# Attention steps taken from two heads in turn and weighed as a pair, and a VectorE update placed ahead of the next head's preparation

## The chip, the cores and the metric

The kernel runs on one core of one Trainium2 chip. It is one program for a whole model: a first block of two layers and a second block of two layers, 512 tokens wide 1024. The metric is the device time of one execution in microseconds (us), the median of several runs. The engines are TensorE (PE in the profile; its weight loads are PEld), VectorE (DVE), ScalarE (ACT), GpSimd (POOL) and SyncE (SP), which here only issues DMAs.

## The reference, cut to what matters

The change lies in the mixer of the second block, which runs once in each of its two layers. The mixer has a convolution (done elsewhere), a differential attention of 6 heads and a gated delta rule of 6 heads. What is computed for them:

```python
def diff_attention(q, k, v, lam_q1, ..., subln_w, layer_idx):   # 6 heads, 2 maps per head, 4 blocks of 128 rows
    ...
    def block(args):
        q_blk, blk = args
        s = jnp.einsum("bqmd,bkmd->bmqk", q_blk, kf)
        ...
        p = jax.nn.softmax(s - slopes[:, None, None] * dist, axis=-1)
        p = p.reshape(B, H, 2, Q_BLOCK, S)
        a = p[:, :, 0] - lam * p[:, :, 1]
        return jnp.einsum("bhqk,bkhe->bqhe", a, vf)

def chunk_gated_delta(q, k, v, g, beta):                        # 6 heads, two directions, chunks of 64
    ...
    decay = jnp.exp(jnp.where(lower, gc[..., :, None] - gc[..., None, :], -jnp.inf))
    A = jnp.where(strict, jnp.einsum("bhncd,bhnsd->bhncs", kb, kc) * decay, 0.0)
    sol = lax.linalg.triangular_solve(A, rhs, left_side=True, lower=True, unit_diagonal=True)
    ...
    def step(state, inp):
        v_new = u_i - jnp.einsum("bhcd,bhde->bhce", w_i, state)
        o = jnp.einsum("bhcd,bhde->bhce", qg_i, state) + jnp.einsum("bhcs,bhse->bhce", aqk_i, v_new)
        state = state * gl_i[..., None, None] + jnp.einsum("bhcd,bhce->bhde", kdec_i, v_new)
```

## The kernel before

`mixer_stage` writes the order of each engine out by hand. Engines run in program order, and semaphores tie them together. The loop goes over 49 slots, t = 7h + lv: for each of the 6 delta heads h it has 7 levels lv, in which the inverse of the triangular matrix is built up by doubling, and a last row of 7 slots (h = 6) that only finishes what is behind. The loop of a slot has, on each engine, pieces of three pipelines:

- **The levels.** TensorE turns the present inverse (`turn`, L3283) and multiplies it with a masked block (`pairs`, L3267). ScalarE copies both results out of PSUM (`turned_copy` L3491, `pairs_copy` L3495). TensorE multiplies the copies (`products`, L3292). VectorE subtracts the product (`update`, L3808 and L3809; L3801 at level 6), and the next slot's `turn` waits for that. GpSimd makes the masked blocks (`masked_level`, L3656).
- **The next head's preparation and the last head's recurrence.** VectorE takes `low` (L3763), `exponents` (L3769 for the first direction, L3772 for the second) and `queries` (L3777) for head h + 1 at levels 2 to 5; ScalarE follows with `decay_exp` (L3478) and `low_exp` (L3472), which stand in its order ahead of the next slot's copies. For head h - 1, TensorE runs `values` (L3318), `results` (L3332, L3337) and `states_seen` (L3303); VectorE `values` (the copy L3823), `states` and `corrected`. `results` of level 4 waits for the copy that VectorE makes at the end of level 3. TensorE runs `before(h, lv)` ahead of `products` and `behind(h, lv)` behind it.
- **The attention steps.** There are 24 steps, one for a head and a block of 128 rows, numbered head by head. Step s begins in slot begins[s] = 7h + 2i + 2. Then, by lag: lag 0 `scores` (L3383, two matmuls from the stacked queries and keys of its head); lag 1 `top` on VectorE and `exps` on ScalarE (L3543); lag 2 `invert`, `rescale` (L3549), `subtract` (L3751); lag 3 `turn_step` (L3393), four transposes in two parts with ScalarE's `copy` between them (L3555); lag 4 `weigh` (L3400), four matmuls of 128x64 weights with 128 columns, and `out` on ScalarE (L3560). `weigh` and the first part of `turn_step` stand between `pairs` and `products`; `scores` and the second part stand behind `products`. Weights of 64 columns fill one half of TensorE's columns: even heads the lower, odd heads the upper, by `half(h)`. fp32 matmuls show as two records each.

The stacked operands lie in two buffers, by h % 2. SyncE fills one with 12 DMAs of 64 KB (L3226), when the scores that read its last content are done: for h >= 2, `sp.wait_ge(scored, 8 * (h - 1))`.

`core.hold` (L242) adds matmuls whose results nobody reads; it stands in slots 1 to 4 and in the last 7.

In the slots of level 5 from head 1 on (t = 12, 19, ...) the weighing of one step and the first transposes of another meet, and the transposes wait for `out`, since both share bank 7.

Of the kernel before, what the change touches and what calls it, by code (L numbers as in the profile page):

```python
# [1066 lines left out]
class Modulation:  # L1067
# [19 lines left out]
    def sum(self, q, n):  # L1087
        return self.core.sb(self.sums[q % len(self.sums)] + n * MOD_W, MOD_W)
# [1688 lines left out]
def u2(core, t):  # L2777
    return core.sb(U0 + t * SEQ, SEQ)
# [330 lines left out]
def mixer_stage(core, nc, a, l, pl):  # L3109
# [22 lines left out]
    ds_bank = lambda d, hh: core.ps[hh, 4, 2 * P + d * HD:2 * P + (d + 1) * HD]  # L3132
    score_bank = lambda m: core.ps[:, 5 + m, :]
    turn_bank = core.ps[:, 7, 0:2 * P]
    weigh_bank = lambda hh: core.ps[hh, 7, 2 * P:3 * P]
    level_of = lambda h, lv: h * LV + lv
    masked_of = lambda h, lv: h * (LV - 1) + lv
    moved_at = lambda h, lv: h * (2 * LV - 1) + 2 * lv + 1
# [47 lines left out]
    def half(h):  # L3186
        return slice((h % 2) * HD, (h % 2 + 1) * HD)
# [1 line left out]
    def order(d):  # L3189
        return range(4) if d == 0 else range(3, -1, -1)  # L3190

    steps = [(h, i) for h in range(6) for i in range(4)]
    N = len(steps)
    slots = LV * (H + 1)
    split_at = {LV - 1: 1, 3 * LV - 1: 2}
# [1 line left out]
    sc = lambda s, c, w=2: core.sb(GX0 + (s % 2) * 8 + c, w)  # L3197
    tiles_of = lambda n, t: u2(core, 4 + 3 * n + t)

    begins = [LV * h + 2 * i + 2 for h, i in steps]  # L3200

    def step_at(t, lag):

        return begins.index(t - lag) if t - lag in begins else None

    kv_bank = lambda b: core.ps[:, (4, 3, 1)[b % 3], :]
    kv_at = lambda b: c4(pl.kt if b < 3 else pl.vt)[:, :, (b % 3) * P:(b % 3 + 1) * P]

    with nc.Block() as block:
        @block.sync  # L3210
        def _(sp):
            sp.dma_start(pl.pairs, core.const("pairs")).then_inc(loads_in, 16)
            sp.dma_start(pl.dist, core.const("dist")).then_inc(loads_in, 16)
            for n, name in enumerate(("diff_lambda_q1_2", "diff_lambda_k1_2", "diff_lambda_q2_2", "diff_lambda_k2_2")):
                sp.dma_start(pl.lamv[:, n * 32:(n + 1) * 32], a[name][l].partition_broadcast(P)).then_inc(loads_in, 16)
            for h in range(H):
                t = h // 2
                sp.wait_ge(pair_low, 2 * t + 2)
                if h >= 2:
                    sp.wait_ge(scored, 8 * (h - 1))  # L3220
                parts = [(pl.high[n].bitcast(F32), tiles_of(n, t)) for n in range(2)]
                for m in range(2):
                    mp = (2 * h + m) % 4
                    for n, (high, low) in enumerate(parts):
                        for place, src in enumerate(((low, high, high), (high, low, high))[n]):
                            sp.dma_start(pl.stack[h % 2][m][n][place * DD:(place + 1) * DD].bitcast(F32),  # L3226
                                         src[mp * DD:(mp + 1) * DD]).then_inc(stack_in[h % 2], 16)

        @block.tensor
        def _(pe):  # L3230
# [154 lines left out]
            def turn_step(s, part):  # L3385
                if part == 0:
                    pe.wait_ge(subtracted, s + 1)
                    if s:
                        pe.wait_ge(out_done, s)
                else:  # L3390
                    pe.wait_ge(turned_copied, 2 * s + 1)
                for j in range(2):
                    mm = nc.tensor.transpose(turn_bank[:, cc(j)], pl.both[s % 2][:, cc(2 * part + j)], core.ident())  # L3393
                mm.then_inc(turned, 1)

            def weigh(s):
                h, i = steps[s]
                pe.wait_ge(turned_copied, 2 * s + 2)
                for j in range(4):
                    mm = nc.tensor.matmul(weigh_bank(half(h)), pl.vt_diff[:, j * DIFF_W + h * HD:j * DIFF_W + (h + 1) * HD],  # L3400
                                          pl.at[s % 2][:, cc(j)], start=(j == 0), stop=(j == 3))
                mm.then_inc(weighted, 1)

            def attend(t, place):

                if place == 0:
                    for s, work in ((step_at(t, 4), weigh), (step_at(t, 3), lambda s: turn_step(s, 0))):
                        if s is not None:
                            work(s)
                else:  # L3410
                    for s, work in ((step_at(t, 0), scores), (step_at(t, 3), lambda s: turn_step(s, 1))):
                        if s is not None:
                            work(s)
# [48 lines left out]
        def _(act):  # L3462
# [88 lines left out]
            def copy(s, part):  # L3551
                act.wait_ge(turned, 2 * s + part + 1)
                if part == 0 and s >= 2:
                    act.wait_ge(weighted, s - 1)
                nc.scalar.activation(pl.at[s % 2][:, two(part)], turn_bank, ACT.Copy).then_inc(turned_copied, 1)  # L3555

            def out(s):
                h, i = steps[s]
                act.wait_ge(weighted, s + 1)
                nc.scalar.activation(u2(core, 4 + h // 2)[half(h), cc(i)], weigh_bank(half(h)), ACT.Copy).then_inc(out_done, 1)  # L3560

            row_exp(0, 0)
            split(0)
# [13 lines left out]
            for t in range(slots):  # L3577
                h, lv = divmod(t, LV)
                if step_at(t, 4) is not None:
                    copy(step_at(t, 4), 1)  # L3580
                if h < H and lv:
                    turned_copy(h, lv)
                    pairs_copy(h, lv)
                    if lv < LV - 1:
                        save(h, lv)
                    else:
                        full(h)
                    if lv == 5 and h < H - 1:
                        near(h + 1)
                if step_at(t, 2) is not None:  # L3590
                    rescale(step_at(t, 2))
                if step_at(t, 4) is not None:
                    out(step_at(t, 4))
                if step_at(t, 3) is not None:
                    copy(step_at(t, 3), 0)
                if step_at(t, 1) is not None:
                    exps(step_at(t, 1))
                if t in split_at:
                    split(split_at[t])
                if lv == 0 and h > 1:  # L3600
                    outputs(h - 2)
                if h < H - 1 and lv in (1, 2, 3):
                    prepare(h + 1, lv - 1)
# [100 lines left out]
        def _(dve):  # L3704
# [106 lines left out]
            def corrected(h, n):  # L3811
                dve.wait_ge(seen, 3 * h + n)
                for d in range(2):
                    R, c = pl.run[d], order(d)[n]
                    rv = R["rv"][h % 2][:, ch(c)]
                    dve.wait_ge(ops_done, 2 * h + d + 1)
                    nc.vector.scalar_tensor_tensor(out=rv, in0=seen_bank(d), scalar=cols(pl.nbge, h, d)[:, c:c + 1], in1=rv,
                                                   op0=ALU.mult, op1=ALU.add).then_inc(rv_done, 1)
# [43 lines left out]
            for t in range(slots):  # L3862
                h, lv = divmod(t, LV)
                ahead = h < H - 1
                if step_at(t, 1) is not None:
                    top(step_at(t, 1))
                if step_at(t, 2) is not None:
                    invert(step_at(t, 2))
                if h:
                    if lv in (0, 2, 5):  # L3870
                        values(h - 1, (0, 2, 5).index(lv) if lv < 5 else 3)
                    if lv in (1, 4):
                        states(h - 1, (0, 2)[lv // 4])
                    if lv == 3:
                        corrected(h - 1, 2)
                if ahead and lv == 2:
                    low(h + 1, 0)
                    exponents(h + 1, 0)
                if ahead and lv == 3:
                    low(h + 1, 1)  # L3880
                    exponents(h + 1, 1)
                if ahead and lv in (4, 5):
                    queries(h + 1, lv - 4)
                if h < H and t:
                    update(h, lv)
                if t == 1:
                    query_gram(0)
                    lambdas_difference()
                if t in (2, 3):
                    queries(0, t - 2)  # L3890
                if step_at(t, 2) is not None:
                    subtract(step_at(t, 2))
                if ahead and lv in (1, 2):
                    differences(h + 1, lv - 1)
                if h:
                    if lv in (1, 4):
                        corrected(h - 1, (1, 3)[lv // 4])
                    if lv == 2:
                        states(h - 1, 1)
                    if lv == 3:  # L3900
                        values(h - 1, 2)
                if ahead and lv == 4:
                    key_gram(h + 1)
                if ahead and lv == 5:
                    query_gram(h + 1)
                if t in split_at:
                    split(split_at[t])
# [129 lines left out]
```

## Time and profile before

| what | value |
|---|---|
| median of 3 runs | 3773.4 us (3767.73 to 3790.59) |
| the profiled execution's own time | 3768.21 us |
| its span | 3766.4 us, 58660 instructions |
| mean granted TensorE clock | 0.989 |
| PE / DVE / ACT / POOL busy | 97% / 57% / 41% / 9% |

The span is the time from the first to the last instruction. The profiled execution lies near the fastest of the runs, 5 us below their median. Clock 1.00 is 2.4 GHz, 0.50 is 1.2 GHz. A matmul's time in the profile goes from its start to its modelled end; consecutive ones overlap, so the distance between starts is what they cost.

### The profile page before, as it was taken

What the parts mean: (1) busy time and instruction counts of PE and PEld (TensorE: products, weight loads), DVE (VectorE), ACT (ScalarE), POOL (GpSimd) and SP (SyncE); (2) the same over time, 40 slices, a digit from 0 to 9 for tenths busy, and PEclk for the clock granted to TensorE, in tenths of its full rate; (3) what the DMA queues carried; (4) which work ended last, traced back from release to release, by engine and by line L of the source; (5) the groups of instructions that cost most, each with busy time, mean ns of one, the idle gap of its engine ahead of it and who ended that gap; (6) DMA issues with size and microseconds to landing.
All of it is one profiled execution on the core that took longest, in us unless ns stands there. A gap on an engine that the chain in (4) does not pass through costs nothing. (4 is left out here: it accounts for less than half of the span.)

```text
span 3766.4 us, 58660 instructions
## 1 busy us (share of the span) xinstructions
PE 3642.5 (97%) x24921; PEld 3014.7 (80%) x24921; DVE 2162.8 (57%) x3353; ACT 1537.2 (41%) x2423; POOL 335.0 (9%) x325
## 2 busy tenths in 40 slices
PE   7999899999999999999999998999999998999998
PEld 4887688888888888878888777777888777778887
DVE  4734766455466444465227776755367867644375
ACT  3224633111354322354226435643266436633364
POOL 0030220000000000000000005410000015310000
PEclk9999999999999999999999999999999999999999
DMA  5530013333212111122323311113232311022231
GB/s 194 176 109 5 7 46 112 124 123 123 87 62 69 62 57 65 65 79 90 100 89 101 91 56 35 28 46 101 79 111 90 91 47 31 20 90 79 90 101 67
DMA packets 262767, 301.24 MB, mean 80 GB/s; under 512 B 9371, under 2 KB 229426, under 8 KB 262514
## 3 DMA queue, kind: packets, MB, share of 16 engines
q1 hardware_dynamic: 260433, 293.41, 24.3%
q8 instruction: 190, 3.11, 0.3%
q10 hardware_dynamic: 2080, 4.19, 0.3%
q14 instruction: 64, 0.52, 0.0%
HBM read 284.14 MB, written 2.10 MB: 76 GB/s over the span
## 5 line engine op out<-in xcount | busy, mean ns | idle before, releaser
L536 PE MATMUL banks<-h_halves,w_halves 128*128 128x512 f32 x3708 | 1370.8, 370 | 14.1 <-DVEq L428 10.6
L538 PE MATMUL banks<-h_halves,w_halves 128*128 128x512 f32 x3708 | 1365.0, 368 | 0.0
L540 PE MATMUL banks<-h_halves,w_halves 128*128 128x512 f32 x3708 | 1359.6, 367 | 0.0
L536 PEld LDWEIGHTS banks<-h_halves,w_halves 128*128 128x128 f32 x3708 | 699.0, 189 | 146.8 <-issue 13.8
L540 PEld LDWEIGHTS banks<-h_halves,w_halves 128*128 128x128 f32 x3708 | 697.5, 188 | 118.5
L538 PEld LDWEIGHTS banks<-h_halves,w_halves 128*128 128x128 f32 x3708 | 698.7, 188 | 115.6 <-issue 1.4
L263 DVE TENSOR_TENSOR w_halves<-work,w_halves 128x2048 fp32r<-128x2048 f32 (+1 forms) x212 | 482.5, 2276 | 486.0 <-ACT w_halves L258 485.9
L258 ACT ACTIVATE w_halves<-work 128x2048 fp32r<-128x2048 f32 (+1 forms) x212 | 401.8, 1895 | 387.4 <-PE banks L540 363.6
L258 ACT ACTIVATE h_halves<-kept 128x512 fp32r<-128x512 f32 (+1 forms) x520 | 332.8, 666 | 282.3 <-PE banks L540 235.6
L263 DVE TENSOR_TENSOR h_halves<-kept,h_halves 128x512 fp32r<-128x512 f32 (+1 forms) x514 | 356.8, 735 | 137.4 <-ACT h_halves L258 136.3
L1130 DVE SCALAR_TENSOR_TENSOR kept<-kept 128x512 f32<-128x512 f32 x280 | 189.8, 749 | 9.9 <-DMA kept<-in_mod_w 9.9
L884 ACT ACTIVATE kept<-banks 128x512 f32<-128x512 f32 x66 | 30.0, 530 | 242.0 <-PE banks L540 242.0
L1510 POOL TENSOR_TENSOR h_halves<-kept,h_halves 128x768 fp32r<-128x768 f32 (+1 forms) x8 | 13.7, 1712 | 1282.3 <-ACT kept L1477 1282.3
L869 ACT ACTIVATE kept<-kept 128x512 f32<-128x512 f32 x64 | 37.6, 632 | 213.9 <-DVE kept L863 213.9
L2480 PE MATMUL banks<-h_halves,w_halves 128*128 128x512 f32 x320 | 119.8, 374 | 1.2 <-DVE h_halves L1484 0.8
L2481 PE MATMUL banks<-h_halves,w_halves 128*128 128x512 f32 x320 | 118.2, 369 | 0.0
L242 PE MATMUL banks<-kept 128*1 128x128 f32 x914 | 113.3, 276 | 4.9 <-DVE work L2294 4.9
L2482 PE MATMUL banks<-h_halves,w_halves 128*128 128x512 f32 x320 | 117.8, 368 | 0.0
L863 DVE SCALAR_TENSOR_TENSOR kept<-banks,kept 128x512 f32<-128x512 f32 x64 | 41.4, 685 | 122.4 <-PE banks L540 122.3
L2498 PE MATMUL banks<-w_halves,h_halves 128*128 128x256 f32 x384 | 108.7, 283 | 0.0
L2497 PE MATMUL banks<-w_halves,h_halves 128*128 128x256 f32 x384 | 108.7, 283 | 0.0
L2496 PE MATMUL banks<-w_halves,h_halves 128*128 128x256 f32 x384 | 108.7, 283 | 0.0
(415 smaller groups left out, 4685.3 us busy)
## 6 DMA issues: line engine op xcount, KB each, us to landing
work<-in_w_ff SPq DMA_DIRECT2D x64, 1024.0 KB, 5.3
work<-in_ffn_w_in SPq DMA_DIRECT2D x44, 1024.0 KB, 5.1
kept<-in_mod_w SPq DMA_DIRECT2D x40, 1024.0 KB, 5.1
work<-in_odd_w_in SPq DMA_DIRECT2D x24, 1024.0 KB, 5.2
work<-in_w_in SPq DMA_DIRECT2D x24, 1024.0 KB, 5.2
work<-in_ffn_w_out SPq DMA_DIRECT2D x16, 1024.0 KB, 5.3
work<-in_even_w_in SPq DMA_DIRECT2D x13, 1024.0 KB, 5.3
work<-in_odd_w_out SPq DMA_DIRECT2D x8, 1024.0 KB, 5.3
```

Source lines behind the costliest of these rows:

```text
L242: self.nc.tensor.matmul(self.ps[0:1, bank, 0:P], self.sb(ONES0, 1), self.ident(), start=True, stop=True)
L258: return core.nc.scalar.activation(dst, src, ACT.Copy)
L263: return core.nc.vector.tensor_tensor(dst, src, high.bitcast(F32), ALU.subtract)
L536: nc.tensor.matmul(o, low[:, k - a, fc], rh[:, tc], start=opens, stop=False, skip_group_check=shared)
L538: nc.tensor.matmul(o, high[:, k - a, fc], rl[:, tc], start=False, stop=False, skip_group_check=shared)
L540: mm = nc.tensor.matmul(o, high[:, k - a, fc], rh[:, tc], start=False, stop=(k == K - 1), skip_group_check=shared)
L1130: ins = nc.vector.scalar_tensor_tensor(out=self.sum(q, n), in0=self.slot(m)[:, k], scalar=c, in1=self.sum(q, n), op0=ALU.mult, op1=ALU.add)
L2480: nc.tensor.matmul(o, low[:, c, fc], rh, start=(c == 0), stop=False)
L2481: nc.tensor.matmul(o, high[:, c, fc], rl, start=False, stop=False)
L2482: mm = nc.tensor.matmul(o, high[:, c, fc], rh, start=False, stop=(c == KD - 1))
L2496: nc.tensor.matmul(o, core.h(c, 1)[:, tc], high[:, c, :], start=(c == 0), stop=False)
L2497: nc.tensor.matmul(o, core.h(c)[:, tc], low[:, c, :], start=False, stop=False)
```

## The change

The 24 steps are numbered so that the two heads of a pair take turns: step s is block i of head 2b + e, in the order b, i, e. The slots in which steps begin are the same numbers as before. An odd step's slot of lag 4 weighs its own and the preceding step: eight matmuls, alternating between the two column halves, and one `out` of 128 partitions in place of two of 64. The slots of lag 4 of even steps (7q + 6, level 6, and 7q + 10, level 3, for q = 0 to 5) have no `weigh` and no `out` any more. Both heads of a pair must be stacked before the second step, and SyncE's wait for a free buffer becomes step (h - 2, 3)'s scores in the new order. On VectorE, `update` moves ahead of `low`, `exponents` and `queries` of the next head, in levels 2 to 5.

```diff
-    weigh_bank = lambda hh: core.ps[hh, 7, 2 * P:3 * P]
+    weigh_bank = core.ps[:, 7, 2 * P:3 * P]
...
-    steps = [(h, i) for h in range(6) for i in range(4)]
+    steps = [(2 * b + e, i) for b in range(3) for i in range(4) for e in range(2)]
...
-    begins = [LV * h + 2 * i + 2 for h, i in steps]
+    begins = [LV * (s // 4) + 2 * (s % 4) + 2 for s in range(N)]
+    weighed_before = lambda s: sum(1 for n in range(1, N, 2) if begins[n] + 4 <= begins[s] + 3)
...
+    def odd_step(t, lag):
+
+        s = step_at(t, lag)
+        return s if s is not None and s % 2 else None
...
-                    sp.wait_ge(scored, 8 * (h - 1))
+                    sp.wait_ge(scored, 2 * steps.index((h - 2, 3)) + 2)
...
             def turn_step(s, part):
                 if part == 0:
                     pe.wait_ge(subtracted, s + 1)
-                    if s:
-                        pe.wait_ge(out_done, s)
+                    if weighed_before(s):
+                        pe.wait_ge(out_done, weighed_before(s))
...
             def weigh(s):
-                h, i = steps[s]
                 pe.wait_ge(turned_copied, 2 * s + 2)
                 for j in range(4):
-                    mm = nc.tensor.matmul(weigh_bank(half(h)), pl.vt_diff[:, j * DIFF_W + h * HD:j * DIFF_W + (h + 1) * HD],
-                                          pl.at[s % 2][:, cc(j)], start=(j == 0), stop=(j == 3))
+                    for n in (s - 1, s):
+                        h, i = steps[n]
+                        mm = nc.tensor.matmul(weigh_bank[half(h)], pl.vt_diff[:, j * DIFF_W + h * HD:j * DIFF_W + (h + 1) * HD],
+                                              pl.at[n % 2][:, cc(j)], start=(j == 0), stop=(j == 3))
                 mm.then_inc(weighted, 1)
...
-                act.wait_ge(weighted, s + 1)
-                nc.scalar.activation(u2(core, 4 + h // 2)[half(h), cc(i)], weigh_bank(half(h)), ACT.Copy).then_inc(out_done, 1)
+                act.wait_ge(weighted, s // 2 + 1)
+                nc.scalar.activation(u2(core, 4 + h // 2)[:, cc(i)], weigh_bank, ACT.Copy).then_inc(out_done, 1)
...
-                if step_at(t, 4) is not None:
-                    out(step_at(t, 4))
+                if odd_step(t, 4) is not None:
+                    out(odd_step(t, 4))
...
+                if h < H and t:
+                    update(h, lv)
                 if ahead and lv == 2:
                     low(h + 1, 0)
                     exponents(h + 1, 0)
...
                 if ahead and lv in (4, 5):
                     queries(h + 1, lv - 4)
-                if h < H and t:
-                    update(h, lv)
```

## Rows read from the trace of the kernel before

**Rows 1.** The page: busy time, share of the span, instructions, by engine.

```profile
PE 3642.5 (97%) x24921; PEld 3014.7 (80%) x24921; DVE 2162.8 (57%) x3353; ACT 1537.2 (41%) x2423; POOL 335.0 (9%) x325
```

**Rows 2.** Windows: length, busy PE, PEld, DVE, ACT, POOL; clock; DMA; the first mixer.

```profile
2268.00:2496.00 228.00, 209.45 (x3781) 166.58 (x3782) 151.31 (x458) 140.01 (x368) 98.52 (x121) 0.97 0.11 26
```

**Rows 3.** Timeline of PE, mixer of the first block: start, duration, line, tile, records.

```profile
349.20 1.09 PE L2013 MATMUL banks<-work,kept 128*64 128x128 f32 x16
```

**Rows 4.** Timeline of PE, head 2, levels 5 and 6; idle time and releaser in brackets.

```profile
2372.05 0.41 PE L3393 MATMUL banks<-kept 128*128 128x128 f32 x2 [0.45 <-ACT kept L3560]
...
2375.95 1.09 PE L3400 MATMUL banks<-work,kept 128*64 128x128 f32 x8
2376.96 0.68 PE L3292 MATMUL banks<-work 64*64 64x64 f32 x16
```

**Rows 5.** Timeline of ACT, head 2, level 6.

```profile
2376.06 0.38 ACT L3495 ACTIVATE work<-banks 128x256 f32<-128x256 f32 x1
```

**Rows 6.** Timeline of PE, head 2, levels 3 and 4.

```profile
2361.71 0.45 PE L3292 MATMUL banks<-work 32*32 32x32 f32 x32
2362.16 0.66 PE L3318 MATMUL banks<-work 128*128 128x64 f32 x4
2363.79 0.45 PE L3283 MATMUL banks<-kept,work 32*32 32x32 f32 x32 [0.97 <-DVE work L3808]
...
2364.92 0.45 PE L3332 MATMUL banks<-work 128*64 128x64 f32 x4 [0.37 <-DVE work L3823]
```

**Rows 7.** Timeline of DVE, head 2, level 3.

```profile
2362.02 0.92 DVE L3763 TENSOR_SCALAR work<-work 128x512 f32<-128x512 f32 x1
2362.86 0.68 DVE L3772 SCALAR_TENSOR_TENSOR work<-work 128x512 f32<-128x512 f32 x1
2363.46 0.27 DVE L3808 TENSOR_TENSOR work<-work,banks 128x128 f32<-128x128 f32 x1
...
2363.86 0.74 DVE L3751 SCALAR_TENSOR_TENSOR kept<-kept 128x512 f32<-128x512 f32 x1
2364.52 0.34 DVE L3823 COPY work<-banks 128x64 f32<-128x64 f32 x2
```

**Rows 8.** Timeline of POOL, head 2, level 3.

```profile
2361.93 0.73 POOL L3656 TENSOR_TENSOR work<-work 128x256 f32<-128x256 f32 x1
```

**Rows 9.** Timeline of DVE, head 5, level 3.

```profile
2458.09 0.29 DVE L3808 TENSOR_TENSOR work<-work,banks 128x128 f32<-128x128 f32 x1 [0.96 <-PE banks L3292]
```

**Rows 10.** Timeline of ACT, head 0, level 3.

```profile
2295.45 0.63 ACT L3478 ACTIVATE work<-work 128x512 f32<-128x512 f32 x1 [0.25 <-DVE work L3772]
```

**Rows 11.** Timeline of PE, the last seven slots, slot 45.

```profile
2483.34 1.09 PE L3400 MATMUL banks<-work,kept 128*64 128x128 f32 x8
2484.36 0.82 PE L242 MATMUL banks<-kept 128*1 128x128 f32 x6
```

**Rows 12.** Windows: head 1 (levels 3 to 4, then 4 to 5), head 2 (3 to 4).

```profile
2323.30:2328.60 5.30, 3.91 (x119) 3.39 (x120) 5.01 (x19) 4.37 (x13) 3.61 (x5) 1.00 0.42 102
2328.60:2338.90 10.30, 10.30 (x97) 8.60 (x96) 5.78 (x16) 3.42 (x10) 5.34 (x7) 0.50 0.01 2
2360.10:2365.40 5.30, 3.95 (x118) 3.35 (x119) 5.01 (x18) 4.08 (x12) 2.97 (x5) 1.00 0.38 91
```

**Rows 13.** Timeline of PE, head 1, levels 4 and 5.

```profile
2328.08 0.45 PE L3332 MATMUL banks<-work 128*64 128x64 f32 x4 [0.37 <-DVE work L3823]
...
2339.73 0.41 PE L3393 MATMUL banks<-kept 128*128 128x128 f32 x2 [0.45 <-ACT kept L3560]
```

**Rows 14.** Timeline of SP's queue: first and last issues of one head's stack.

```profile
2354.95 1.82 SPq L3226 DMA_DIRECT2D p_halves<-kept  x3
...
2363.09 0.58 SPq L3226 DMA_DIRECT2D p_halves<-work  x1
```

**Rows 15.** DMA issues by line: count, KB each, median us from issue to landing.

```profile
p_halves<-kept SPq DMA_DIRECT2D x48, 64.0 KB, 2.0
```

**Rows 16.** Timeline of PE: the scores of slots 13 and 16.

```profile
2346.56 0.73 PE L3383 MATMUL banks<-p_halves 96*128 96x512 f32 x2
...
2358.07 0.73 PE L3383 MATMUL banks<-p_halves 96*128 96x512 f32 x2
```

More of the change, by code:

```diff
@@ L3406, in attend @@
                 if place == 0:
-                    for s, work in ((step_at(t, 4), weigh), (step_at(t, 3), lambda s: turn_step(s, 0))):
-                        if s is not None:
-                            work(s)
+                    if odd_step(t, 4) is not None:
+                        weigh(odd_step(t, 4))
+                    if step_at(t, 3) is not None:
+                        turn_step(step_at(t, 3), 0)
                 else:
@@ L3553, in copy @@
                 if part == 0 and s >= 2:
-                    act.wait_ge(weighted, s - 1)
+                    act.wait_ge(weighted, s // 2)
                 nc.scalar.activation(pl.at[s % 2][:, two(part)], turn_bank, ACT.Copy).then_inc(turned_copied, 1)
@@ L3591, in _ @@
                     rescale(step_at(t, 2))
-                if step_at(t, 4) is not None:
-                    out(step_at(t, 4))
+                if odd_step(t, 4) is not None:
+                    out(odd_step(t, 4))
                 if step_at(t, 3) is not None:
```

## The prediction, made before the result was known

> **What bounds the kernel now.** I read the page first: TensorE is busy for 97% of the span [rows 1]. The windows of the first mixer say how much of that the change can reach: a stage of 228 us, with TensorE busy 209 of them, at a mean clock of 0.97 [rows 2]; the second mixer is a like stage. 1% of the kernel is 37.7 us, so an eighth of one mixer. About 1% is also what a measurement of this kernel can tell from no change. Then I read the timeline slot by slot, on all engines, for one head, and asked at each `products` and each `turn` what it had waited for.
>
> Levels 4, 5, 6, 0, 1 and the start of 2 go mostly at TensorE's own pace: its instructions follow each other, and what is taken out there shortens the slot, until ScalarE's copies come last. Level 3 and the start of level 4 do not. There TensorE stands for 0.97 us until `update` is done, and 0.37 us more until VectorE has made the copy L3823 [rows 6]. VectorE has no gap in that stretch: L3763, L3772, `update`, `subtract` and the copy follow end to end [rows 7]. So in level 3 of heads 1 to 4, which all have this form, VectorE sets the pace.
>
> **The weighing itself.** A pair takes eight matmuls in place of twice four. The first block's mixer already weighs two heads in alternating column halves: 16 records in 1.09 us [rows 3]. One head here takes 8 records in the same 1.09 us [rows 4]. I take the pair at 1.09 us: the weighings that stay (levels 1 and 5) cost what they did, and 12 weighings in each mixer are gone. The other bound is that nothing overlaps, 1.0 us more at each of 24 pairs. The Trainium skill, "TensorEngine Tiling (Array Packing)", section "Key Properties", says that changing the tiling mode drains the engine. Modes alternate between neighbours in both kernels, and by that rule a removed weighing would give back a drain too; no row here separates one, and the sum leaves it out.
>
> **Level 6, six in each mixer.** `products` started at 2376.96, behind the weighing that began at 2375.95 [rows 4]. Without it the next thing to wait for is ScalarE's copy of the pairs, which ended at 2376.44 [rows 5]. So 0.5 us of the 1.0 come out, 12 x 0.5 = 6.0 us. Bounds 0.4 and 1.0 each.
>
> **Level 3, heads 1 to 4, eight in all.** `products` would start 1.0 us earlier than 2361.71 [rows 6], but VectorE is still at work until 2362.02 [rows 7]. `update` now comes first there and is done at 2362.4, so TensorE turns and pairs at once. Then it meets `results`, which waits for the copy L3823. Its place in VectorE's order is unchanged, behind `low`, `exponents`, `update` and `subtract` in whichever order, and these add up to the same 2.5 us. So the wait for `update` becomes a wait for the copy, and the gain of both halves of the change is nothing here. One small term is left: L3763 ran beside GpSimd's L3656 from 2362.02 to 2362.66 and took 0.92 us [rows 7, 8]; 0.4 us later it meets it for 0.24 us only. I take 0.3 us each (0 to 0.4): 2.4 us.
>
> **Level 3, head 5, two in all.** No next head is prepared; VectorE waited 0.96 us for `products` [rows 9], and gets them a weighing earlier: 2 x 0.95 = 1.9 us.
>
> **The last seven slots.** TensorE runs from the weighing into fillers without a gap [rows 11]: 2 x 1.0 = 2.0 us.
>
> **Head 0.** ScalarE's `decay_exp` already waited 0.25 us for `exponents` [rows 10], and the next slot's two copies stand behind it. `exponents` now stands behind `update`, which waits for `products`: 0.4 us of `update` and 0.1 to 0.4 us of waiting. I charge 0.5 us in each mixer, 1.0 us (0 to 2).
>
> **The rest of the moved order, at nothing.** In levels 2, 4 and 5, `update` comes up to 0.6 us sooner, but TensorE did not wait for it; `queries` comes later, and its readers are a slot away. ScalarE loses twelve `out` of 0.27 us in each mixer; nothing waits for them but the transposes of level 5 [rows 4], and that one stays.
>
> **SyncE's loads.** Heads 0 and 1 are stacked back to back before slot 4, as the 24 issues already stand. For heads 2 and 4 the release moves from slot 8 (22) to slot 13 (27), while the first use stays at slot 16 (30). From the end of the scores of slot 13 to those of slot 16 there were 10.8 us [rows 16]. The load takes 8.1 us from first to last issue and 2.0 us to land [rows 14, 15], 10.1 us. That fits by 0.6 us, where it had several slots to spare before, and the odd head's load queues behind it with about the same margin. TensorE would stand with everything behind `scores`. For heads 2 to 5 of both mixers I charge 1 us in sum (0 to 5).
>
> Together: -6.0 - 2.4 - 1.9 - 2.0 + 1.0 + 1.0 = -10.3 us, if the clock does what it did.
>
> **The clock.** I don't think it will. In head 1 the granted clock fell to 0.50 (1.2 GHz) at 2328.6 and stayed there for 10.3 us [rows 12]; what TensorE had done before was the level 3 pattern, 3.91 us busy of 5.3. In head 2 the same stretch with 3.95 us of 5.3 passed at 1.00. The second mixer shows the same: a fall behind level 3 of head 1, none in heads 2 to 4. So two of eight such stretches fall, and the others stand close to it. The change takes the 1.0 us of the weighing out of just this stretch while its length, VectorE's, stays: idle time rises from 1.35 to about 2.4 us, and what is left is mostly 32x32 tiles. The price is in the rows: from `results` of level 4 to the first transposes of level 5, head 1 took 11.65 us [rows 13] and head 2 took 7.13 us [rows 4, 6], so 4.5 us. I expect five of the other six stretches to fall: +22.5 us. The Trainium skill, "TensorE: Matmul & The Clock Gate", section "HAM oscillation — how this bites in real kernels", tells of kernels whose engine drops to the lower clock again and again through idle gaps between bursts; this speaks against taking work out of a stretch that another engine sets, and by it the further falls come. In rows 12 one stretch agrees and one does not.
>
> **The sum.** The profiled execution took 3768.2 us. 3768.2 - 10.3 + 22.5 = 3780.4 us. The median of the runs lies 5.2 us above the profiled time; I add half of that and forecast 3783 us.
>
> **Rivals.**
> - The clock holds: TensorE's idle time in level 3 rises, but the clock falls only where it did. For it: three of four heads passed at 1.00 with a quarter of the stretch idle, and head 0 has longer gaps. Against it: the near equality of two stretches of which one fell [rows 12]. It gives 3768 - 10 = 3758 to 3763 us. Chance 0.32.
> - The stacks come late: from a load time of 10.8 us on, every further us is paid at heads 2 and 4, and again for heads 3 and 5, at the worst 1.2 us at eight places, about 8 us above the rest: 3768 to 3772 us with the clock as before. Chance 0.08.
> - The eight matmuls do not overlap: +1.0 us at the 24 pairs against the sum of -10.3 us, and fuller stretches for the clock: about 3782 us. Rows 3 speak against it. Chance 0.04.
> - Slower by over 1%: the clock falls in all eight stretches and, head 0 being slower too, in both of its, and once more in each head, since a stretch at 1.2 GHz moves what comes after it: 14 further falls x 4.5 = 63 us, minus 10. It decides from some ten further falls on. 3811 us and above. Chance 0.04.
> - Faster by over 1% would need four times the sum: 0.01.
> - My forecast, 3 to 7 further falls, 3771 to 3790 us: 0.51.
>
> The likeliest case gives the time. Its own range is 3771 to 3792 us. The range for 8 in 10 has to take in the case in which the clock holds, and on the other side eight falls with late stacks: 3756 to 3797 us. In chances: slower by over 1% 0.05, faster by over 1% 0.01, within 1% 0.94.
>
> **What would show it.** In the timeline of the changed kernel: L3400 with x16 in 1.09 us at levels 1 and 5 only; L3292 of level 6 starting right at the end of L3495; in level 4 of heads 1 to 4 no wait of L3283 for L3808, but some 1.5 us of L3332 for L3823; L3383 of slots 16 and 30 waiting for the queue if the stacks are late. In the windows: clock 0.50 behind level 3 of heads 2 to 4. I am wrong if VectorE's stretch in level 3 gets shorter by more than 0.5 us, or if the mixers' mean clock stays at 0.97.

## The result, and the profile after

The changed kernel is slower: 3792.3 us median (3787.4 to 3810.76, 20 runs) against 3773.2 us (3767.5 to 3790.6, 20 runs), ratio 1.0043, 95% interval 1.0031 to 1.0054. The forecast was 3783 us, range 3756 to 3797. Its profiled execution has a span of 3791.1 us against 3766.4.

The page's line of busy times answers to [rows 1], the windows of both mixers to [rows 2].

```profile
PE 3654.7 (96%) x24921; PEld 3022.2 (80%) x24921; DVE 2158.8 (57%) x3353; ACT 1531.9 (40%) x2399; POOL 336.5 (9%) x325
```

```profile
2271.00:2509.00 238.00, 212.08 (x3788) 168.17 (x3789) 151.36 (x463) 138.18 (x359) 99.48 (x121) 0.90 0.10 25
3108.00:3344.00 236.00, 213.99 (x3737) 168.95 (x3734) 145.09 (x453) 132.67 (x349) 93.83 (x115) 0.86 0.09 22
```

ScalarE has 24 instructions fewer, TensorE the same number. The mixers' mean clock went from 0.97 to 0.90 and 0.86. From the scores of slot 2 to the first matmul of the next stage the first mixer took 206.4 us before and 213.8 after, the second 205.9 and 219.8. So 21.3 of the 24.7 us are there. The other 3.4 us lie ahead of the first mixer, in code that did not change. They look like a difference between executions: the scores of slot 2 of the first mixer start at 2291.2 us in the profiled execution of the kernel before, and at 2292.2 to 2298.4 us in those of all other kernels here.

TensorE's timeline for levels 3 to 6 of head 2 answers to [rows 4, 6]. `products` is now L3298, `values` L3324, `turn` L3289, `results` L3338, `weigh` L3407, `scores` L3389.

```profile
2361.52 0.73 PE L3389 MATMUL banks<-p_halves 96*128 96x512 f32 x2
...
2365.61 0.66 PE L3324 MATMUL banks<-work 128*128 128x64 f32 x4 [1.01 <-DVE work L3825]
2366.20 0.45 PE L3289 MATMUL banks<-kept,work 32*32 32x32 f32 x32
...
2367.97 0.69 PE L3338 MATMUL banks<-work 128*64 128x64 f32 x4 [0.91 <-DVE work L3831]
...
2377.46 1.09 PE L3407 MATMUL banks<-work,kept 128*64 128x128 f32 x16
2379.02 0.41 PE L3399 MATMUL banks<-kept 128*128 128x128 f32 x2 [0.47 <-ACT kept L3568]
...
2383.47 0.68 PE L3298 MATMUL banks<-work 64*64 64x64 f32 x16 [0.48 <-ACT work L3503]
```

`turn` no longer waits for `update`; `results` waits 0.91 us for VectorE's copy, and `values`, which stands ahead of `turn`, waits 1.01 us for `corrected` (L3825): 1.9 us idle where 1.34 were. The pair takes 16 records in 1.09 us. In level 6, `products` waits for ScalarE's copy. VectorE's timeline of level 3 answers to [rows 7]: the same instructions end to end, `update` (L3816) first, the copy (L3831) last.

```profile
2365.09 0.47 DVE L3825 SCALAR_TENSOR_TENSOR work<-banks,kept,work 128x64 f32<-128x64 f32 x2
2365.47 0.28 DVE L3816 TENSOR_TENSOR work<-work,banks 128x128 f32<-128x128 f32 x1
...
2365.86 0.52 DVE L3771 TENSOR_SCALAR work<-work 128x512 f32<-128x512 f32 x1
2366.31 0.68 DVE L3780 SCALAR_TENSOR_TENSOR work<-work 128x512 f32<-128x512 f32 x1
2366.91 0.74 DVE L3759 SCALAR_TENSOR_TENSOR kept<-kept 128x512 f32<-128x512 f32 x1
2367.57 0.34 DVE L3831 COPY work<-banks 128x64 f32<-128x64 f32 x2
```

The windows up to the fall of the clock and behind it, head 2 and head 3, answer to [rows 12] (the clock is the third number from the end).

```profile
2361.50:2366.70 5.20, 3.79 (x165) 3.11 (x168) 4.32 (x15) 3.99 (x12) 3.12 (x4) 1.00 0.34 80
2366.70:2376.90 10.20, 9.29 (x119) 7.56 (x107) 6.44 (x19) 4.18 (x11) 5.26 (x6) 0.50 0.12 29
2398.90:2404.20 5.30, 3.18 (x131) 2.71 (x120) 5.01 (x20) 4.31 (x12) 3.55 (x5) 1.00 0.01 3
2404.20:2414.40 10.20, 10.20 (x101) 8.49 (x101) 5.23 (x15) 3.49 (x10) 5.28 (x7) 0.50 0.01 2
```

The clock fell behind level 3 of heads 1, 2, 3 and 4, in both mixers: eight falls, two before. In the second mixer it was low once more in head 0, for 23.9 us from 3131.2 on.

In heads 1, 2 and 4 of both mixers, six of the eight, the clock was low before the wait of `results` began: in head 2 from 2366.7 on, while that wait runs from 2367.1 to 2367.97. By then TensorE had missed the weighing and stood for 1.4 us of 5.2 us, most of it in front of `values`; in head 2 of the kernel before it stood for 1.35 us of 5.3 us, and the clock stayed at 1.00 [rows 12]. So the 1.9 us of both waits are not what brought the clock down, and the idle time alone does not tell the stretches that fell from those that passed.

### The profile page after: what moved, and what is told of

Read it like the earlier page. It is cut to its first block and busy times, and to the rows that moved or that the text cites. A ratio compares the mean times of both kernels' runs of the same rounds, so it can differ in the third digit from the quotient of the medians.

```text
span 3791.1 us, 58634 instructions
## 1 busy us (share of the span) xinstructions
PE 3654.7 (96%) x24921; PEld 3022.2 (80%) x24921; DVE 2158.8 (57%) x3353; ACT 1531.9 (40%) x2399; POOL 336.5 (9%) x325
## 5 line engine op out<-in xcount | busy, mean ns | idle before, releaser
L536 PE MATMUL banks<-h_halves,w_halves 128*128 128x512 f32 x3708 | 1370.5, 370 | 14.0 <-DVEq L428 10.6
L536 PEld LDWEIGHTS banks<-h_halves,w_halves 128*128 128x128 f32 x3708 | 699.0, 189 | 145.9 <-issue 13.7
L1510 POOL TENSOR_TENSOR h_halves<-kept,h_halves 128x768 fp32r<-128x768 f32 (+1 forms) x8 | 13.7, 1713 | 1282.6 <-ACT kept L1477 1282.6
```

What stands on the lines that cost most here:

```text
L536: nc.tensor.matmul(o, low[:, k - a, fc], rh[:, tc], start=opens, stop=False, skip_group_check=shared)
```

## The experiments

Two theories. **Clock:** TensorE's missing microsecond in level 3 makes the granted clock fall there, and the falls are the whole loss. **Order:** the new waits (for VectorE's copy, for `exponents`, for the stacks) are the loss, and the clock goes along. The table has every run; "falls" are stretches at 0.50 that begin behind level 3 of heads 1 to 4, of eight in a profiled execution.

The falls are counted in one execution of each kernel, and executions differ. The mean granted clock of every execution bears the counts out: 0.971 to 0.980 in the changed kernel and 0.969 to 0.977 in e2; 0.988 to 0.991 in e1, 0.987 to 0.991 in e8 and 0.986 to 0.991 in e4; 0.978 to 0.991 in 85 executions of the kernel before, whose profiled execution, at 0.989, lies above its median of 0.987. It thus shows less low clock than most executions of that kernel have.

| kernel | weighing in level 3 | fillers | falls | median us | ratio to before, interval |
|---|---|---|---|---|---|
| before | yes | no | 2 | 3773 to 3776 | |
| changed | no | no | 8 | 3792.3 | 1.0043 (1.0031 to 1.0054) |
| e1 changed | no | 4 and 3 | 0 | 3760.4 | 0.9952 (0.9934 to 0.997) |
| e2 pairs only | no | no | 8 | 3808.2 | 1.0076 (1.005 to 1.0102) |
| e3 `update` only | yes | no | 1 | 3777.5 | 1.0002 (0.9984 to 1.002) |
| e4 before | yes | 3 and 1 | 0 | 3763.7 | 0.9973 (0.9956 to 0.999) |
| e5 changed | no | 4 and 3, more | 0 | 3751.1 | 0.994 (0.9917 to 0.9962) |
| e6 as e1, one head after the other | no | 4 and 3 | 0 | 3767.1 | 0.9976 (0.9956 to 0.9995) |
| e7 order only | yes | no | 3 | 3790.0 | 1.0043 (1.0016 to 1.0069) |
| e8 changed | no | 4 | 0 | 3756.5 | 0.995 (0.9929 to 0.997) |
| e9 as e7 | yes | 3 and 1 | 0 | 3762.7 | 0.9969 (0.9957 to 0.9981) |
| e10 as e2 | no | 4 and 3, more | 0 | 3753.0 | 0.9945 (0.9929 to 0.9961) |
| e11 changed | no | 2 | 3 | 3785.3 | 1.0032 (1.0011 to 1.0053) |
| e12 changed | no | 4, more | 0 | 3754.8 | 0.9953 (0.9934 to 0.9973) |

**e1, the changed kernel with fillers.** A filler is a matmul of one weight column whose result nobody reads, as `core.hold` has them, in a free part of bank 7.

```diff
+            def fill(n):
+                for _ in range(n):
+                    nc.tensor.matmul(core.ps[0:1, 7, 3 * P:4 * P], core.sb(ONES0, 1), core.ident(), start=True, stop=True)
...
                         pairs(h, lv)
+                    if 1 <= h <= 4 and lv == 4:
+                        fill(3)
                     before(h, lv)
...
                         products(h, lv)
+                    if 1 <= h <= 4 and lv == 3:
+                        fill(4)
                     behind(h, lv)
```

> The changed kernel with fillers on TensorE where it now stands idle: four filler matmuls behind `products` of level 3 and three ahead of `results` of level 4, for heads 1 to 4 (about 1.0 and 0.8 us, in gaps of 1.0 and 0.9 us). Clock theory: the granted clock stays at 1.00 behind level 3 of heads 1 to 4; the seven or eight falls there are gone, at 3.5 to 4.5 us each, so 3792 - 30 = 3758 to 3768 us, below the kernel before (ratio 0.996 to 0.999). Rival, in which the new waits in the order (for VectorE's copy, for `exponents`, for the stacks) carry the loss and the clock only goes along: the fillers fill idle time and nothing else moves, 3790 to 3795 us.

Measured 3760.4 us: 32 us off the changed kernel and 0.5% under the one before, by adding work. TensorE's timeline in head 2, fillers at L3433:

```profile
2363.13 1.03 PE L3433 MATMUL banks<-kept 128*1 128x128 f32 x8
2364.21 0.66 PE L3324 MATMUL banks<-work 128*128 128x64 f32 x4
...
2365.49 0.81 PE L3433 MATMUL banks<-kept 128*1 128x128 f32 x6
2366.58 0.45 PE L3338 MATMUL banks<-work 128*64 128x64 f32 x4 [0.28 <-DVE work L3839]
```

and the same windows as above:

```profile
2360.10:2365.40 5.30, 4.85 (x181) 3.79 (x180) 4.41 (x15) 4.09 (x12) 3.13 (x4) 1.00 0.34 80
2365.40:2375.60 10.20, 9.45 (x160) 7.68 (x146) 7.46 (x24) 6.93 (x20) 6.21 (x8) 1.00 0.12 29
```

From the scores of slot 16 to `results` of level 4 it is 6.46 us, as in the changed kernel (2361.52 to 2367.97): the fillers bought no time there. They kept the clock behind it. The order theory gave 3790 to 3795 us and is refuted as the cause of the loss. Elsewhere the clock was not quite held: in e1 it fell once in head 5, for 10.2 us, and in head 0 of both mixers.

**e2, pairs only:** `update` back behind `low`, `exponents` and `queries`, the rest as in the changed kernel.

```diff
-                if h < H and t:
-                    update(h, lv)
                 if ahead and lv == 2:
...
                     queries(h + 1, lv - 4)
+                if h < H and t:
+                    update(h, lv)
```

> Steps in pairs and weighed side by side, `update` back behind the next head's preparation. Clock theory: the weighing is still missing from level 3 and VectorE still sets its length, so the clock falls behind level 3 of nearly all of heads 1 to 4 in both mixers, 3784 to 3793 us; TensorE's idle time is in front of `turn` again and not in front of `results`. Rival, in which the moved `update` is what costs: 3760 to 3770 us, faster than before by the 6 to 10 us of the removed weighings.

Measured 3808.2 us, above my 3784 to 3793. All eight stretches fell, four for 13.7 us and one for 30.7 us; in head 0 of the first mixer the clock was low for 23.9 us more. TensorE's timeline in head 2:

```profile
2372.65 0.66 PE L3324 MATMUL banks<-work 128*128 128x64 f32 x4 [1.01 <-DVE work L3825]
...
2374.28 0.65 PE L3289 MATMUL banks<-kept,work 32*32 32x32 f32 x32 [0.97 <-DVE work L3816]
```

The move of `update` is not what loses: without it the kernel is 16 us slower still. That the order of the steps or the removed weighing is, this run can't tell apart, since it has both (see e7 to e9). That a low stretch gets longer in this form than in the changed kernel I had not foreseen, and nothing here explains it.

**e3, `update` only:** the diff of e2 the other way round, on the kernel before.

> Only `update` ahead of the next head's preparation; steps and weighing as before. Clock theory: level 3 keeps its weighing and its 1.3 us of idle time, now in front of `results`; two or three falls behind level 3 as before; 2 us won beside GpSimd, 1 to 2 us lost in head 0: 3770 to 3778 us. Rival, in which the moved `update` costs: 3783 us and above.

Measured 3777.5 us, ratio 1.0002, one fall. The move alone changes nothing that shows; the interval leaves room for 0.2%, 7 us, either way.

**e4, the kernel before with fillers.** Three ahead of `turn` of level 4 (with a wait for `out` of the step weighed in level 3, since both use bank 7), one ahead of `results`.

```diff
+                    if 1 <= h <= 4 and lv == 4:
+                        pe.wait_ge(out_done, step_at(t - 1, 4) + 1)
+                        fill(3)
                     if h < H and lv:
                         turn(h, lv)
...
+                    if 1 <= h <= 4 and lv == 4:
+                        fill(1)
                     before(h, lv)
```

> The kernel before with fillers at the same place: three ahead of `turn` of level 4 and one ahead of `results`, heads 1 to 4 (gaps of 0.97 and 0.37 us). Clock theory: the one fall behind level 3 of head 1 in each mixer goes, 2 x 4.5 us, so 3762 to 3768 us (ratio 0.997 to 0.999). Rival, in which a fall behind level 3 costs little since VectorE sets the pace there: 3772 to 3776 us.

Measured 3763.7 us, in the range, 10 us under the kernel before. The traces price one fall: from the scores of slot 9 to those of slot 16, with the fall of head 1 between them, the kernel before took 36.45 us and e4 31.96 us, so 4.5 us; the second mixer has 36.46 and 31.95.

```profile
2321.62 0.73 PE L3383 MATMUL banks<-p_halves 96*128 96x512 f32 x2
```

```profile
2324.74 0.73 PE L3383 MATMUL banks<-p_halves 96*128 96x512 f32 x2
...
2356.70 0.74 PE L3383 MATMUL banks<-p_halves 96*128 96x512 f32 x2
```

The first line is of the kernel before, whose slot 16 is in [rows 16]; the others are of e4. e4 is also the fair base for the change: with the clock held behind level 3 in both, e1 (3760.4) and e8 (3756.5) are 3 to 7 us faster than e4.

**e5, more fillers.** Those of e1, and also in heads 0 and 5, slot 1 and slot 8; the edit is shown against e1.

```diff
+                    if t == LV + 1:
+                        core.hold(2, 6)
                     if h < H and lv:
                         turn(h, lv)
...
-                    if 1 <= h <= 4 and lv == 3:
-                        fill(4)
+                    if lv == 3 and h < H:
+                        fill(4 if h < 5 else 2)
+                    if t == 1:
+                        fill(6)
```

> The changed kernel with the fillers of the first experiment and more of them: four behind `products` of level 3 of head 0, two of head 5, six behind `products` of slot 1, six ahead of `turn` of slot 8. Clock theory: the falls left in the two mixers (slot 7 to 8, head 0, head 5) go too, 1.5 to 5 us each, up to 1 us lost at head 5's filler: 3752 to 3757 us, the fastest of all, 0.994 to 0.9955 of the time before. Rival, in which those falls cost nothing or the fillers cost what they save: 3759 to 3763 us.

Measured 3751.1 us, the fastest of all, 0.6% under the kernel before. No fall is left in either mixer of its profiled execution.

**e6, one head after the other.** As e1, with the loops over j and n in `weigh` exchanged.

> As the first experiment (changed kernel with fillers in levels 3 and 4), but a pair's eight matmuls run all four of one head and then all four of the other. If the two column halves work side by side only when they alternate: 16 records of L3407 take 2.1 us in place of 1.09, and 24 pairs cost 1.0 us each on TensorE's path, 3780 to 3786 us against 3760. If order doesn't matter, because the halves never overlapped or overlap at any distance: 3758 to 3763 us.

Measured 3767.1 us, 7 us over e1: neither of my two numbers. TensorE's timeline, head 2, level 6:

```profile
2384.85 1.53 PE L3407 MATMUL banks<-work,kept 128*64 128x128 f32 x16
2386.31 0.68 PE L3298 MATMUL banks<-work 64*64 64x64 f32 x16
```

The group takes 1.53 us, where alternating takes 1.09 and two weighings one after the other would take 2.1. Record by record, the fifth record of the first head starts at 2385.283, and the first of the second head at 2385.289. So the second half began when four records of the first were on their way, and then both ran at their own pace. 24 pairs x 0.44 us are 10.6 us at most; 6.7 showed.

**e7, the order only,** and **e9, the same with the fillers of e4.** On the kernel before:

```diff
-    steps = [(h, i) for h in range(6) for i in range(4)]
+    steps = [(2 * b + e, i) for b in range(3) for i in range(4) for e in range(2)]
...
-    begins = [LV * h + 2 * i + 2 for h, i in steps]
+    begins = [LV * (s // 4) + 2 * (s % 4) + 2 for s in range(N)]
...
-                    sp.wait_ge(scored, 8 * (h - 1))
+                    sp.wait_ge(scored, 2 * steps.index((h - 2, 3)) + 2)
```

> Only the order of the steps is changed (two heads in turn, both stacks early, SyncE's later release); every step is weighed alone in its own slot, and `update` is where it was. Clock theory: level 3 keeps its weighing, falls as before, 3770 to 3778 us. Rival, in which the late stacks cost: TensorE waits for p_halves at slots 16 and 30, and the time is 5 to 8 us above the kernel before.

> The kernel with only the order of the steps changed, with the fillers that the kernel before got in the fourth experiment (three ahead of `turn` of level 4, one ahead of `results`). If falls of the clock are why the order alone came out slower (three of 20 us each in its trace): they go, and the time is that of the kernel before with fillers, 3762 to 3767 us, at most 2 us more for late stacks. If the order itself costs: 3775 us and above.

e7 took 3790.0 us, 14 us over the kernel before and as slow as the changed kernel by its ratio. That spoke for the order theory, but its stacks were late only twice, by 1.3 us together, far from 14. Its windows in head 2:

```profile
2356.30:2361.60 5.30, 3.61 (x129) 2.91 (x116) 5.23 (x18) 4.16 (x12) 3.25 (x5) 1.00 0.34 83
2361.60:2382.10 20.50, 19.99 (x172) 16.45 (x173) 9.91 (x25) 8.04 (x23) 8.93 (x12) 0.50 0.02 5
```

Three falls of 20.5 us each, behind the same waits of 0.97 and 0.37 us as in [rows 6]. e9 decides it: with fillers the same order takes 3762.7 us, e4's time, and behind the same place the clock stays at 1.00:

```profile
2363.50:2384.00 20.50, 19.01 (x289) 15.64 (x289) 13.88 (x42) 14.07 (x39) 12.95 (x16) 1.00 0.03 8
```

The order costs nothing that shows beyond the clock. Why its falls last 20.5 us where those of [rows 12] lasted 10.3 is left open. So is how the loss of the changed kernel divides between the new order and the removed weighing: without fillers the order alone lost about as much time with three falls as the whole change with eight.

**e8, fillers of level 3 only,** **e11, two of them in place of four,** and **e12, e5 without those of level 4.**

> The changed kernel with four fillers behind `products` of level 3 of heads 1 to 4 only: as much TensorE time as the removed weighing, in the same place, and nothing in the second gap ahead of `results`. Clock theory with the removed microsecond as the cause: most falls behind level 3 go, 3760 to 3768 us. If only the second gap (0.9 us, made by the moved `update`) matters: they stay, 3785 to 3792 us.

> The changed kernel with two fillers in place of four behind `products` of level 3, half of the TensorE time that the weighing took there. If the stretch stands close to what keeps the clock, as the kernel before suggests: some of the eight stretches fall, three to five, 3768 to 3780 us. If any filler breaks the gap up and that is enough: 3756 to 3760 us, as with four.

> The fillers of the fifth experiment without those of level 4. The eighth experiment held the clock behind level 3 without them: 3749 to 3753 us, level with the fifth or up to 2 us faster. If the second gap needs them once the first experiment's other falls are gone: a fall or two of 4.5 us come back, 3754 to 3760 us.

e8: 3756.5 us, no fall in eight. The removed microsecond, put back as fillers, is enough; the second gap needs none. It is still there, and the clock stays at 1.00 behind it:

```profile
2361.81 1.03 PE L3433 MATMUL banks<-kept 128*1 128x128 f32 x8
...
2365.25 0.45 PE L3338 MATMUL banks<-work 128*64 128x64 f32 x4 [1.01 <-DVE work L3837]
```

```profile
2364.10:2374.30 10.20, 8.72 (x152) 7.27 (x138) 7.47 (x24) 6.93 (x20) 6.23 (x8) 1.00 0.12 29
```

e11: 3785.3 us and three falls in eight, with 0.5 us put back, and a further one at head 5. It is slower than I expected. In its trace the clock also fell in head 0 of both mixers; and that execution took 3775.6 us, 10 us under the median, so the others will have had more low clock (their mean granted clock goes down to 0.977, where it has 0.983). e12: 3754.8 us, some 4 us over e5, with overlapping intervals; its one low stretch in the mixers, 6.8 us, is in head 0.

**e10, pairs only with all fillers.** As e2, with e5's, those of level 4 ahead of `turn`.

> Pairs weighed side by side, all fillers of the fifth experiment (those of level 4 now ahead of `turn`), and `update` in its old place. With the clock held, what is left of the move of `update` shows: my sum had 2 us won beside GpSimd and 1 us lost in head 0, so 3751 to 3754 us against 3751. If the move is worth more (TensorE gets `turn` and `pairs` done in the gap): 3757 us and above.

3753.0 us against 3751.1: the move of `update` is worth at most a few microseconds, and the intervals don't separate it from nothing. e10 and e12 also say what the weighing in pairs is worth when the clock is alike: they are 8 to 10 us under e9, which weighs each step alone (3753.0 and 3754.8 against 3762.7), and the clock was at 0.50 for 77, 76 and 73 us in their profiled executions. The prediction's sum without the clock was -10.3 us.

**Late stacks** showed as waits of `scores` for the DMA in eight kernels (e1, e2, e5, e7 to e11), once or twice in each, for 0.6 to 1.5 us in sum; in the changed kernel there is none. A late stack can cost more than its wait: in e10 the scores of slot 4 of the second mixer waited 1.38 us, the clock fell 1.1 us behind them and stayed low for 17.1 us. Another of them, in e1, slot 16 of the second mixer:

```profile
3182.53 0.73 PE L3389 MATMUL banks<-p_halves 96*128 96x512 f32 x2 [1.03 <-DMA p_halves<-work]
```

## Why the prediction was right, point by point

The forecast was 3783 us, 10 us above the kernel before, and the change measured 19 us: the direction and the cause were right, the amount about half.

- **The pair at 1.09 us:** right, 16 records in 1.09 us. The bound for no overlap, 1.0 us more, was not reached even by one head after the other, which took 0.44 us more.
- **Level 6, 0.5 us each:** right. `products` waits 0.48 us for the copy, and slots 39 to 41, the same place in head 5, where the clock stood at 1.00 before and after, shrank by 0.45 us.
- **Level 3, heads 1 to 4, nothing but 0.3 us:** right in size. With the clock at 1.00, slots 16 to 23, 23 to 30 and 30 to 37 of the first mixer took 0.84, 0.71 and 0.84 us less in e1 than before: 0.8 us, which is 0.45 of level 6 and some 0.3 left for level 3. L3771 took 0.52 us, where L3763 took 0.92 [rows 7]. Where TensorE stands was half right: the text has it turn at once and then wait some 1.5 us in front of `results`. It waits 0.91 us there, and 1.01 us in front of `values`, which the text did not have.
- **Level 3, head 5, 0.95 us, and the last slots, 1.0 us:** slots 37 to 39 took 7.31 us and then 6.31; from slot 43 to the next stage 19.77 and then 18.76. Both right.
- **Head 0, 0.5 us lost:** slots 2 to 4 took 0.42 us longer. `decay_exp` waited 0.83 us instead of 0.25:

```profile
2299.91 0.63 ACT L3486 ACTIVATE work<-work 128x512 f32<-128x512 f32 x1 [0.83 <-DVE work L3780]
```

- **Stacks, 1 us:** none late in the changed kernel's trace, 0 to 1.5 us of waiting in the experiments. Right in size, for the waiting alone.
- **The clock:** the decisive step was right, and its size too small. The text expected idle time of 2.4 us; `values` and `results` show 1.9, and in six of eight stretches the clock fell before the second of these waits. What e1 and e8 bear out is the removed microsecond of work, not the sum of the waits. Six further stretches fell, not five. From slot 16 to 23, 23 to 30 and 30 to 37 the first mixer took 3.06, 3.86 and 3.04 us longer; with the 0.8 us won these falls cost 3.9, 4.6 and 3.9 us, 4.1 in the mean, not 4.5. Six make 24.7 us where I had 22.5. Head 1's falls lasted 13.7 us and not 10.2: 1.2 us more in sum. And head 0 took 0.1 us more in the first mixer and 6.3 us in the second, which the forecast did not have. What was won elsewhere is 11.1 us: 8 x 0.8 in heads 1 to 4 and 4.7 in head 5 and the last slots. That sum is 24.7 + 1.2 + 6.4 - 11.1 = 21.2 us, against 21.3 measured in the two mixers. The profiled execution passed the sum of 3780.4 us by 12.5 us; 6.4 of them are head 0 and 3.4 the time ahead of the first mixer, neither of them in the forecast, and only some 3 us are errors in its own terms.
- **What the clock step cites.** The Trainium skill, "TensorE: Matmul & The Clock Gate", section "HAM oscillation — how this bites in real kernels", tells of one kernel whose gaps are waits for DMA, longer than the work between them. No gap in level 3 here is like that: the longest single wait ahead of a fall was 1.2 us, for VectorE. The section does not foretell these falls; the step rests on [rows 12] and the runs.
- **A slip of scale:** 37.7 us, 1% of the kernel, is a sixth of one mixer of 228 us, not an eighth. And less than 1% could be told: 20 runs of each kernel show 0.4% with an interval of 0.1% to either side.
- **Head 0 of the second mixer.** The low stretch followed a pause of TensorE in the midst of `pairs`, for which the profile shows no waited-for event:

```profile
3131.06 0.33 PE L3273 MATMUL banks<-work 32*32 32x32 f32 x13 [1.61 <-issue]
```

The same place has pauses of 0.2 to 1.0 us in some other traces, that of before among them. Whether the change has a part in it is not settled. In e5 the clock stayed at 1.00 behind pauses of 0.70 and 0.77 us in that part, which had more fillers; none of 1.6 us occurred there.

## What to carry to other kernels

Where another engine sets the length of a stretch, as VectorE did in level 3, TensorE work taken out of it wins next to nothing and can lose the clock for what comes next; look at the granted clock behind each such stretch first, and at how many like ones already fall. A few fillers in the gap turned a change of +0.4% into one of -0.5%, with those in further gaps -0.6%, and brought 0.3% to the kernel before. An experiment on a schedule near that margin should be run with fillers and without: order alone looked like +14 us, and no cost showed once the clock was held.

## What the runs showed of the hardware

- With the weighing in level 3 the granted clock stayed at 1.00 in 18 of 24 stretches (before, e3, e7); without it in 0 of 16 (changed, e2). 0.5 us of one-column fillers in its place brought that to 5 of 8 (e11), 1.0 us to 8 of 8 (e8), with a wait of 1.01 us left behind them.
- The same instructions behind the same waits of 0.97 and 0.37 us in head 2 passed at 1.00 in the kernel before and fell to 0.50 in e7. What tells the two apart no run here shows.
- One such fall cost 4.5 us (slots 9 to 16, before against e4).
- Fillers of one weight column and 128 moving columns kept the clock at 1.00 in all eight stretches, as the weighing's matmuls of 64 weight columns did in most of them.
- Stretches at 0.50 behind level 3 of heads 1 to 4 lasted 10.2 to 30.7 us, in e11 6.8 us once.
- The two column halves of TensorE take their matmuls in parallel also when they don't alternate: in e6 the second half's started when the fifth record of the first did, 1.53 us for 16 records.
